# One level of Strassen's algorithm for the second feed-forward product of a two-layer transformer kernel

## What is computed

```python
def squared_relu_mlp(h, w1, w2):
    return jnp.square(jax.nn.relu(h @ w1)) @ w2
...
x = x + mod_l[5] * squared_relu_mlp(modulate(x, norm2_g[layer], ...), w_ff1[layer], w_ff2[layer])
```

## Time and profile before

| what | value |
|---|---|
| median of three runs | 2229.66 us |
| profiled execution, its own time | 2232.24 us |
| its span, first to last instruction | 2230.4 us |
| mean granted clock of TensorE, of full speed | 0.960 |
| TensorE busy with matmuls | 2058.7 us, 92% |
| VectorE, ScalarE, GpSimd busy | 1016.9, 764.1, 694.3 us |

### The profile page before, as it was taken

The page is one execution under the profiler, slowest core; times in us unless marked ns, Lnnn a source line. Parts: engine busy times, 40 slices in busy tenths (PEclk is TensorE's granted clock), DMA queues, the critical chain, the costliest instruction groups (busy, mean ns, idle before and its releaser), DMA issues.

```text
span 2230.4 us, 31947 instructions
## 1 busy us (share of the span) xinstructions
PE 2058.7 (92%) x13264; PEld 1723.8 (77%) x13264; DVE 1016.9 (46%) x1746; ACT 764.1 (34%) x1263; POOL 694.3 (31%) x566
## 2 busy tenths in 40 slices
PE   4899898989989999999999988998999888999998
PEld 3777786777877788888888877777787777778787
DVE  4555447836865521312212354445857755121122
ACT  2333324535454421312223233323454364232231
POOL 0232212013732232232223313213024523444452
PEclk8899998989999999999999998998999989999999
DMA  8320000452421122112111122010242312322321
GB/s 262 79 65 20 29 30 20 152 133 73 153 76 48 48 64 69 57 57 70 63 57 57 57 53 72 20 38 20 93 124 95 114 57 76 95 95 86 102 79 74
DMA packets 178352, 169.08 MB, mean 76 GB/s; under 512 B 29392, under 2 KB 174880, under 8 KB 178080
## 3 DMA queue, kind: packets, MB, share of 16 engines
q1 hardware_dynamic: 177408, 163.89, 24.2%
q10 hardware_dynamic: 800, 3.15, 0.4%
HBM read 159.15 MB, written 2.10 MB: 72 GB/s over the span
## 4 chain that ended last, share of the span: by engine, by line
PE 78%; DVE 11%; ACT 4%; issue 3%; DMA 2%; SPq 2%; POOL 1%; DVEq 0%; ACTq 0%; POOLq 0%
PE gp L893 54%; PE sp L1126 3%; PE sp L1277 3%; PE gp L1163 2%; PE tp L1143 2%; PE gp L947 2%; SPq L728 1%; DMA raw<-in_w_mod 1%; PE sp L1117 1%; PE gp L917 1%; DVE small L2229 1%; PE op L1143 1%; PE op L1163 1%; PE sp L1024 1%; PE gp L919 1%
## 5 line engine op out<-in xcount | busy, mean ns | idle before, releaser
L804 POOL TENSOR_TENSOR wlo<-raw,whi 128x512 fp32r<-128x512 f32 x386 | 517.1, 1370 | 1264.6 <-ACT whi L1440 1264.4
L893 PE MATMUL gp<-xhi,whi 128*128 128x512 f32 (+1 forms) x1416 | 514.8, 364 | 30.4 <-DVE xlo L2005 21.6
L893 PE MATMUL gp<-xhi,wlo 128*128 128x512 f32 (+1 forms) x1416 | 502.5, 355 | 0.0
L893 PE MATMUL gp<-xlo,whi 128*128 128x512 f32 (+1 forms) x1408 | 501.2, 356 | 0.0
L893 PEld LDWEIGHTS gp<-xhi,whi 128*128 128x128 f32 x1416 | 274.3, 194 | 75.7 <-issue 19.2
L1440 ACT ACTIVATE whi<-raw 128x2048 fp32r<-128x2048 f32 (+1 forms) x100 | 187.4, 1874 | 360.7 <-PE gp L893 352.4
L893 PEld LDWEIGHTS gp<-xhi,wlo 128*128 128x128 f32 x1416 | 273.2, 193 | 38.9
L893 PEld LDWEIGHTS gp<-xlo,whi 128*128 128x128 f32 x1408 | 272.6, 194 | 38.1 <-issue 1.5
L893 PE MATMUL gp<-hhi,whi 128*128 128x512 f32 (+1 forms) x752 | 270.0, 359 | 9.6 <-issue 5.0
L893 PE MATMUL gp<-hlo,whi 128*128 128x512 f32 (+1 forms) x752 | 268.5, 357 | 0.0
L893 PE MATMUL gp<-hhi,wlo 128*128 128x512 f32 (+1 forms) x752 | 268.4, 357 | 0.0
(11 more groups left out here) (395 smaller groups left out, 3253.6 us busy)
## 6 DMA issues: line engine op xcount, KB each, us to landing
raw<-in_w_ff SPq DMA_DIRECT2D x64, 1024.0 KB, 5.3
raw<-in_w_mod SPq DMA_DIRECT2D x48, 1024.0 KB, 5.3
raw<-in_w_in SPq DMA_DIRECT2D x20, 1024.0 KB, 5.3
raw<-in_w_in SPq DMA_DIRECT2D x24, 256.0 KB, 4.6
bias<-e SPq DMA_DIRECT2D x96, 32.0 KB
raw<-in_w_out SPq DMA_DIRECT2D x12, 256.0 KB, 3.0
xin<-in_x ACTq DMA_DIRECT2D x1, 2048.0 KB, 9.8
raw<-in_w_out SPq DMA_DIRECT2D x16, 128.0 KB, 3.5
```

What stands on the lines that cost most here:

```text
L804: nc.gpsimd.tensor_tensor(wlo[:, s % 2, ks, :], raw[:, index[splits[s]] % 2, ks, :], whi[:, s % 2, ks, :].bitcast(F32), ALU.subtract)\
L893: mm = pe.matmul(out, lhs, rhs, start=(i == 0 and j == 0), stop=(i == KT - 1 and j == 2))
```

## The change

In both layers the hidden width is now taken in eight chunks of 512 (`ST_CHUNKS`). A chunk has two `ff1` units as before and then two units `st`, each a 512x512 block of `w_ff2` (again 1 MB). Such a block is multiplied by Strassen's algorithm in its form with shared sums: the block is cut into 2x2 quarters by the parity of its k tile (`c`) and of its output tile (`r`), the hidden values by the parity of the hidden tile (`ct`) and by the half of the tokens. Seven products (`ST_STEPS`) take the place of eight. Four sums of weight quarters are made in place in `raw` (`st_sum`: by VectorE for the first unit of a chunk, by GpSimd for the second), four sums of hidden values in place in `nsq` (`mixed`, VectorE). A step has two k tiles and two output tiles, so 12 matmuls, each with 384 tokens in layer 0 and 256 in layer 1. Sums of products are formed by leaving a bank's value, which VectorE has meanwhile added to `xT`, and accumulating the next step on it. Three pairs of banks (of `sp`, `tp`, `op`) take turns.

The high and low parts of the block, with its sums, are seven pieces of 128x512 (`fb_hi`, `fb_lo`), in one buffer each: piece b of a unit is written only when step b of the unit before has been multiplied. In layer 0 the last chunk has one `st` unit and two conventional `ff2` units with four k tiles each; the second of these is the closing unit.

The core of the diff:

```diff
@@ dense_order
+        if l in ST_LAYERS:
+            for q in range(ST_CHUNKS):
+                for j in range(2):
+                    whole(("ff1", l, q, j))
+                for j in range(st_units(l, q)):
+                    groups.append((("st", l, q, j), None, None))
+            if l < DEPTH - 1:
+                whole(("ff2", l, ST_CHUNKS - 1, 2))
+                closing(("ff2", l, ST_CHUNKS - 1, 3))
+            continue
@@ build
+        ST_SOURCE = ((0, 0), (0, 1), (0, 0), (0, 0), (1, 0), (1, 1), (0, 1))
+        ST_ADD_OF = {2: 2, 3: 4, 4: 1, 6: 3}
+        ST_TARGET = ((0, 0), (0, 0), (1, 0), (1, 1), (1, 1), (1, 0), (0, 1))
+        ST_BANK_BEFORE = {0: (-1, 1), 1: (-1, 5), 2: (0, 0), 3: (-1, 6), 4: (0, 2), 5: (0, 3), 6: (0, 4)}
+        ST_READY = (1, 2, 3, 4, 5, 6, 2)
@@ sync
                     if w[0] == "mod":
                         wait_used(sp, w)
+                    elif w[0] == "st":
+                        sp.wait_ge(st_lo, ST_STEPS * (st_no[w] + 1))
                     else:
                         sp.wait_ge(lo_done, LO_PARTS * (split_no[w] + 1))
@@ gpsimd
+            def st_lower(u):
+                v = ST_STEPS * st_no[u]
+                sums = {0: (0,), 1: (1,), 2: (2,), 3: (3,)} if u[3] else {}
+                for b in range(ST_STEPS):
+                    for n in sums.get(b, ()):
+                        st_sum(pool, nc.gpsimd, u, n)
+                    pool.wait_ge(st_hi, v + b + 1)
+                    nc.gpsimd.tensor_tensor(fb_lo[:, b, :, :, :], st_block(u, *ST_SOURCE[b]), fb_hi[:, b, :, :, :].bitcast(F32), ALU.subtract)\
+                      .then_inc(st_lo, 1)
...
                     low(s)
+                if u[0] == "ff1" and u[1] in ST_LAYERS:
+                    _, l, q, j = u
+                    if j == 0 and q:
+                        st_lower(("st", l, q - 1, 1))
+                    if j == 1:
+                        st_lower(("st", l, q, 0))
+                        if q == ST_CHUNKS - 1 and st_units(l, q) == 2:
+                            st_lower(("st", l, q, 1))
@@ tensor
+            def strassen(u):
...
+                for steps in (((0, 1),) if j == 0 else ((0,), (1,))) + ((2,), (3,), (4,), (5,), (6,)):
+                    for m in range(2):
+                        for step in steps:
+                            if m == 0:
+                                pe.wait_ge(st_lo, ST_STEPS * v + step + 1)
+                            if j == 0:
+                                pe.wait_ge(*upto(l, "h_split", 6 * (2 * q + m) + ST_READY[step]))
+                            for pair in range(2):
+                                if m == 0:
+                                    unit, event = ST_BANK_BEFORE[step]
+                                    if v + unit >= 0:
+                                        pe.wait_ge(st_out, 2 * ST_STEPS * (v + unit) + 2 * event + pair + 1)
...
@@ scalar
+            def block_high(u, b):
+                v = st_no[u]
+                if b == 0:
+                    act.wait_ge(landed[index[u] % 2], landed_at[u])
+                if v:
+                    act.wait_ge(st_done, 2 * ST_STEPS * (v - 1) + 2 * b + 2)
+                if b in ST_ADD_OF:
+                    act.wait_ge(st_added[u[3]], st_adds[u] + ST_ADD_OF[b])
+                nc.scalar.activation(fb_hi[:, b, :, :, :], st_block(u, *ST_SOURCE[b]), ACT.Copy).then_inc(st_hi, 1)
+
+            def feed_forward_st(l):
+                act.wait_ge(*upto(l, "xn2", 2 * KT))
+                for b in range(3):
+                    block_high(("st", l, 0, 0), b)
+                for q in range(ST_CHUNKS):
+                    for j in range(2):
+                        u = ("ff1", l, q, j)
+                        for ct in range(2):
+                            for c in chunks_of(u):
+                                if c[0] == ct and not (u in SEG_MAJOR and c in chunks_of(u)[:2]):
+                                    relu(l, q, j, c)
+                            tile_high(l, q, j, ct)
+                            if j == ct == 0:
+                                for b in range(3, ST_STEPS):
+                                    block_high(("st", l, q, 0), b)
+                        mixed_high(l, q, j)
+                        if j == 0:
+                            after_unit(u)
+                    if st_units(l, q) == 2:
+                        for b in range(ST_STEPS):
+                            block_high(("st", l, q, 1), b)
+                    after_unit(("ff1", l, q, 1))
+                    if q < ST_CHUNKS - 1:
+                        for b in range(3):
+                            block_high(("st", l, q + 1, 0), b)
...
@@ vector
+            def feed_forward_st(l):
+                for q in range(ST_CHUNKS):
+                    for n in range(3):
+                        st_sum(dve, V, ("st", l, q, 0), n)
+                    for j in range(2):
+                        u = ("ff1", l, q, j)
+                        for ct in range(2):
+                            for c in chunks_of(u):
+                                if c[0] == ct:
+                                    a, b = SEGS[c[1]]
+                                    wait_read(dve, None, N(u, c))
+                                    V.tensor_tensor(nsq[:, ct, a:b], nsq[:, ct, a:b], nsq[:, ct, a:b], ALU.mult).then_inc(ls(l, "h_sq"), 1)
+                            tile_low(l, q, j, ct)
+                            if j == ct == 0:
+                                st_sum(dve, V, ("st", l, q, 0), 3)
+                        mixed(l, q, j)
+                    if l < DEPTH - 1 and q == ST_CHUNKS - 1:
+                        lambda_dots(l + 1)
+                    for j in range(st_units(l, q)):
+                        st_add_back(("st", l, q, j))
+                if l < DEPTH - 1:
+                    for k in range(1, 4):
+                        accumulate(l + 1, 1, k, T)
+                    prepare(l + 1)
...
```

More of the change, by code:

```diff
@@ L251, in dense_order, with st_units @@
                 for j in range(4):
[L252 to L255, removed]
-    return groups
+                    whole((kind, l, q, j))
+    return groups
+def st_units(l, q):
+    return 1 if l < DEPTH - 1 and q == ST_CHUNKS - 1 else 2
 COLS = {"DAq": 0, "DAk": 256, "DAv": 512, "HGq": 768, "HGi": 1024, "HGg": 1280, "HGf": 1536,
@@ L268, in build @@
     for u, c, banks in dense_order():
+        if c is None:
+            units.append(u)
+            continue
         b = banks[0] if len(banks) == 1 else 1 - last_gp
@@ L278, in build @@
     index = {u: i for i, u in enumerate(units)}
-    splits = [u for u in units if u[0] != "mod"]
+    splits = [u for u in units if u[0] not in ("mod", "st")]
     split_no = {u: i for i, u in enumerate(splits)}
+    strassens = [u for u in units if u[0] == "st"]
+    st_no = {u: i for i, u in enumerate(strassens)}
+    st_adds = {u: 4 * sum(w[3] == u[3] for w in strassens[:i]) for i, u in enumerate(strassens)}
     def unit_dmas(u):
@@ L863, in start_group, with dense @@
                     pe.wait_ge(bank_free[group_bank[n]], group_turn[n])
-            def dense(u, *cs, ready=None, part=range(KT)):
+            def dense(u, *cs, ready=None, part=None):
                 s = split_no[u] % 2
+                end = k_tiles(u)
+                part = part or range(end)
                 first = cs[0] == chunks_of(u)[0]
@@ new lines, in st_add_back @@
+            def st_add_back(u):
+                _, l, q, j = u
+                base = 2 * ST_STEPS * st_no[u]
+                h = st_half(l)
+                for step in range(ST_STEPS):
+                    row, half = ST_TARGET[step]
+                    for pair in range(2):
+                        k = 4 * j + 2 * pair + row
+                        dve.wait_ge(st_done, base + 2 * step + pair + 1)
+                        if step in ST_AFTER:
+                            dve.wait_ge(st_out, base + 2 * ST_AFTER[step] + pair + 1)
+                        lo, hi = h * half, h * half + h
+                        for a, b, col in ((lo, min(hi, LAT), 0), (max(lo, LAT), hi, 1)):
+                            if a < b:
+                                ins = V.scalar_tensor_tensor(out=xT[:, k, a:b], in0=st_bank(u, step, pair)[:, a - lo:b - lo],
+                                                             scalar=mods[:, l, 40 + k, col:col + 1], in1=xT[:, k, a:b],
+                                                             op0=ALU.mult, op1=ALU.add)
+                        ins.then_inc(st_out, 1)
@@ L2620, in _ @@
                              .then_inc(ls(l, "h_split"), 1)
-                    if q == 3 and not last:
-                        add_and_norm(("ff2", l, q), 5, l, l + 1, 1)
-                        continue
                     for j in range(4):
```

214 lines of the change are left out of this document (171 added, 43 removed).

## The result

| | kernel before | changed kernel |
|---|---|---|
| median of the runs | 2229.11 us (4 runs, 2228.38 to 2230.45) | **2375.64 us** (4 runs, 2370.19 to 2387.13) |
| ratio, 95% interval | | **1.0663** (1.0624 to 1.0703) |
| profiled execution / its span | 2232.24 / 2230.4 us | 2374.6 / 2372.5 us |
| mean granted clock of TensorE | 0.960 | 0.926 |

The change makes the kernel 6.6% slower. The forecast was 2352 us, so the direction and the place were right and the size 24 us too small.

A forecast was written before the change was run, and what follows sets the result against it. TensorE was taken to bound the kernel before, and two waits between engines to outweigh its saving. Profiled 2232.2 + 29 (layer 0) + 93.5 (layer 1) = 2354.7, less 2.6 to the median: 2352 us; range 2285 to 2405.

The forecast's parts named there:

- what TensorE saves: Both layers' 512x512 blocks: fewer matmul columns save 32 us in layer 0 and 20 in layer 1, together 52 us.
- First wait: TensorE at step 2 waits for VectorE to add step 0's bank: 4.0 us per layer 0 chunk, plus 2.2 slow clock.
- +2.3, seven times: Layer 0's chunks except the last: each 70.5 us against 68.2, together +16 us.
- Between the layers: From layer 0's last block to layer 1: `prepare` and accumulations delay `ff2` additions, +5.4 us; closing norm +3.
- Second wait, the ring: Layer 1's weight feed through two `raw` slots: one turn takes 58 us a chunk against 45.3, layer 1 +93.5 us.
- the five links: Layer 1's turn: load and copy 7.4, hidden values 9.1, GpSimd's pieces 14.9, load and copy 7.4, next chunk's part 19.1 us.
- TensorE as the bound: Rival for both layers: TensorE stays the bound and all else hides, 2178 us, faster; chance 0.06.
- no change: Rival for both layers: both waits shorter than worked out, layer 0 gains what layer 1 loses; chance 0.04.
- Little interference: Rival: GpSimd and VectorE hardly disturb each other, layer 1's turn 51.7 us, 2292 us (2309 with layer 0 at +29); chance 0.2.
- Full interference: Rival: VectorE and GpSimd exclude each other for whole instructions, layer 1's turn 64 us, 2399 us in all; chance 0.2.
- (b): Layer 1: hidden values of ff1(q,1) on ScalarE and VectorE, 9.1 us with interference, two sums 0.4 longer; VectorE alone 6.4.
- rival 2: Full interference: each of seven VectorE instructions in (b) waits 0.63 us for GpSimd; 2399 us; chance 0.2.

The follow-up runs named there:

- e2: Changed kernel, with VectorE adding step 0's banks in the middle of `mixed`, behind its second and third sum: 2341.81 us, 1.0498 of the kernel before.
- e3: Changed kernel, with ScalarE's copy of the ff1(q+1,0) weights behind the hidden values of ff1(q,1): 2385.32 us, 1.0707 of the kernel before.
- e14: Strassen in layer 0 only, e11's and e2's orders, shorter way between layers, squares before copy, first chunk's pieces and sums behind hidden values: 2218.65 us, 0.9954 of before.
- e5: e3, with ScalarE's pieces 2 and up and VectorE's sums 1 and 2 behind the first hidden tile: 2361.22 us, 1.0599 of the kernel before.
- e8: e3, with ScalarE's pieces 2 to 6 and VectorE's sums 1 to 3 behind all hidden values of ff1(q,0): 2404.72 us, 1.0796 of before.
- e11: e3, with GpSimd doing all of st(q,1) before the low part of ff1(q+1,0): 2329.58 us, 1.0444 of the kernel before.

## Right and wrong, step by step

- **What bounds the kernel, and what TensorE saves: right.** 384-column matmuls start 0.18 us apart, 256-column ones 0.12; with nearly all waits gone, e2's chunk of layer 0 is 65.2 us, against 64.0 worked out without any wait. The saving of 4.2 us a chunk is real and smaller than one wait at step 2 with what follows it.
- **First wait: right, sizes a little off.** Its wait was 4.65 us for 4.0 and the slow matmuls cost about 2.0 for 2.2, the mean of some 2.5 and 1.5 us by turns. The period came out at 70.0 for 70.5. e2 shows the cause.
- **Layer 0's first chunk: the step that failed.** The forecast priced all eight chunks alike but for the last: "+2.3, seven times". The first one lost 14.1. It has no cover: ScalarE is at the norm until 749, its pieces wait for sums and its relus for the pieces, and then it waits for the load of ff1(1,0) ahead of the relus of ff1(0,1). SyncE issues that load at 765.13, when st(0,0)'s last low piece has ended at 765.11. The same links as in layer 1's ring therefore show once in layer 0, though TensorE hides them later. e3 shows the part of the load: its one edit puts the copy behind the relus, and the 8.85 us fall to 5.47. e14 shows the part of the order.
- **Between the layers: mis-sized.** +12.8 was forecast and +16.4 measured. The wait for the first addition was nearly right (6.83 for 7.1). The loss of cover for the norm was taken as +3, with 5.6 as the upper end; the two waits are 3.25 and 3.14 where 0.47 and nothing stood, +5.9.
- **Second wait, the ring: right in its links and lengths,** 59.0 us for 58, each link within 0.4. Layer 1 lost 10.7 us more than forecast: 6.3 in the six middle chunks by that 1.0, 2.7 in the first, where TensorE waits 3.8 us for `nsq`, and 1.7 in the last. **Incomplete in its paths:** the five links were taken for the only way round. e3, e5 and e8 stay 0.5 to 1.1 us below it, and e11 shows that what held them is a second way through GpSimd's list: with both of its edits it gets to 53.9. Whether GpSimd's edit would do it alone, no run shows.
- **The rivals.** TensorE as the bound (2178 us) is out in both layers by its waits, and with it no change. Little interference, a ring of 51.7, is out by 59.0. Full interference, a ring of 64, did not come either, though interference was stronger than before. A group by form in layer 1's feed-forward, VectorE's squares (xcount | busy, mean ns of one):

```profile
L2336 DVE TENSOR_TENSOR nsq<-nsq 128x512 f32<-128x512 f32 x30 | 40.7, 1356 | 56.9 <-ACT nsq L1658 56.8
```

They took 1.36 us where the earlier trace rows have 0.78. The four sums of (b), 2.75 us together (1.80 in e3), are not lengthened alike. Two of the four, in the chain in order of time (start us, us, what):

```profile
2109.30 1.39 DVE nsq L2296
...
2110.72 0.44 DVE nsq L2296
```

The first starts while GpSimd works on its own sum (2108.69 to 2110.40) and ends 0.29 us after it; the other three find GpSimd idle and take 0.44 each. By the Trainium skill (page "SBUF — State Buffer", section "SBUF: two separate sides") such instructions of the two engines exclude each other for their whole length. The trace agrees: of the squares, low parts and sums of the changed kernel that start while a GpSimd subtraction or sum has more than 0.1 us to go, all 99 of 128x512 end 0.54 to 0.55 us after it, and all 34 of 128x256 end 0.28 to 0.29 us after it, however long it still had to go. VectorE's additions to `xT`, which read one operand from a PSUM bank, take 0.47 to 0.49 us with GpSimd busy or idle. So what rival 2 supposed of the two engines is right, and its price was wrong: it let all seven instructions of (b) pay 0.63, 4.4 us, and three of the four sums met nobody; (b) was 3.0 us above the 6.4 of VectorE alone. The forecast case came close to (b) by other shares than it gave, with two sums 0.4 us longer where one was 0.95 longer, and its reason against rival 2, a mean of 0.78, fits the exclusion too: in the kernel before, the squares of layer 1 took 0.69 us where they met no GpSimd instruction, 0.75 where 0.20 us of one were left, and 1.29 where 0.74 were. The exclusion did not decide the period: in e3 the squares of ff1(q,1) run at 0.69 us, and it is 58.2.

## To carry to other kernels

A change that takes work off the busiest engine is worth its full time only while the other engines' programs let it: write down each engine's list in program order and follow one buffer slot around it (free, load, copy, split, use, free). If that ring is longer than the busy engine's new period, it sets the time, and moving an item on one engine alone may only swap the path, as in e3 to e8. Price the first chunk and the last by themselves, since they have no cover; here they were 30 of layer 0's 41 us.

## What was not expected of the hardware

- TensorE's clock after a wait of 4.65 us: granted 0.50 for the next 9 to 10 or 16 to 17 matmul intervals, by turns from chunk to chunk, with the same work before it and the same wait. After 0.43 us (e2) it did not fall. The price of one and the same wait varies between 1.4 and 2.6 us.
- A VectorE instruction on two operands in SBUF that starts beside a GpSimd instruction ends a fixed 0.55 us (128x512) or 0.28 us (128x256) after the other has ended, and its row in the profile is longer by the wait: a sum of 0.44 us took 1.39. GpSimd's sum that starts beside VectorE's low part took 1.71 us for 1.28. What a short instruction pays thus depends on how much of the other's instruction is left, and a mean over many hides it.
